# Three projection tiles taken group by group beside the first norm, squares and small loads ahead of the weights

## What is computed

```python
def rmsnorm(x, g):
    xf = x.astype(jnp.float32)
    y = xf * lax.rsqrt(jnp.mean(xf * xf, axis=-1, keepdims=True) + NORM_EPS)
    return (y * g.astype(jnp.float32)).astype(x.dtype)
...
    h = rmsnorm(x, g_pre)
    proj = h @ w_in
    u, q, k, v, o, gi, gf, ga, gb = jnp.split(proj, IN_SPLITS, axis=-1)
    y_a = jax.nn.gelu(s5_ssm(u, lam_re, lam_im, b_re, b_im, c_re, c_im, d, log_dt))
...
    dt = jnp.exp(log_dt.astype(jnp.float32))[:, None]
    mag = jnp.exp(lam_re * dt)
    ab_re = mag * jnp.cos(lam_im * dt)
    ab_im = mag * jnp.sin(lam_im * dt)
```

## Time and profile before

| | |
|---|---|
| time, median of 3 runs | 3489.06 us (3487.95 to 3490.17) |
| the profiled execution | 3492.63 us, span of its core 3490.8 us |
| PE busy | 3255.0 us, 93% of the span |
| DVE busy | 1745.0 us, 50% |
| ACT busy | 1203.0 us, 34% |
| chain that ended last | PE 80%, DVE 12%, ACT 5% |

### The profile page before, as it was taken

One profiled execution on the slowest core, in us unless ns is written; L12 is line 12 of the kernel. 1 busy time (PEld: TensorE's weight loads), 2 busy tenths in 40 slices (PEclk: granted clock), 3 DMA queues, 4 the chain that ended last, 5 costly groups with the idle time before them and its releaser, 6 DMA issues.

```text
span 3490.8 us, 55107 instructions
## 1 busy us (share of the span) xinstructions
PE 3255.0 (93%) x23686; PEld 2709.5 (78%) x23686; DVE 1745.0 (50%) x3048; ACT 1203.0 (34%) x2065; POOL 75.8 (2%) x124
## 2 busy tenths in 40 slices
PE   6899988889999999999999898978888999999998
PEld 4788877769878888888777776767677788888887
DVE  7656252345574243446765545454545653434355
ACT  4233353452543221224533222433434431212133
POOL 0000000001000000000000000000000000000000
PEclk9999999999999999999999999989899999999999
DMA  2111121224322111123443122000002221111133
GB/s 102 68 62 65 65 92 61 74 89 131 139 95 86 55 41 52 38 76 127 148 167 120 65 70 83 11 29 29 11 20 91 85 96 62 47 50 46 51 97 109
DMA packets 85234, 262.28 MB, mean 75 GB/s; under 512 B 10208, under 2 KB 10336, under 8 KB 84864
## 3 DMA queue, kind: packets, MB, share of 16 engines
q1 hardware_dynamic: 73056, 217.78, 18.8%
q0 software_dynamic: 7040, 23.16, 1.9%
q10 hardware_dynamic: 4896, 17.84, 1.3%
HBM read 216.51 MB, written 42.21 MB: 74 GB/s over the span
## 4 chain that ended last, share of the span: by engine, by line
PE 80%; DVE 12%; ACT 5%; issue 2%; DMA 1%; DVEq 0%; SPq 0%; POOL 0%; ACTq 0%; POOLq 0%
PE ps L127 77%; DVE HB L161 2%; PE ps L130 2%; PE ps L126 2%; DVE w_lo L161 1%; ACT L140 1%; ACT w_hi L158 1%; DVE HB L171 1%; ACT m_D L140 1%; DVE r_t L161 1%; DVE r_in L161 0%; DVE C L171 0%; DMA w_raw<-in_w_u 0%; DVE r_Xa L161 0%; DMA m_D<-mq 0%
## 5 line engine op out<-in xcount | busy, mean ns | idle before, releaser
L161 DVE TENSOR_TENSOR w_lo<-w_raw,w_hi 128x1024 fp32r<-128x1024 f32 (+3 forms) x353 | 393.5, 1115 | 388.3 <-ACT w_hi L158 386.1
L127 PE MATMUL ps<-XHA,w_hi 128*128 128x264 f32 (+3 forms) x1456 | 474.5, 326 | 24.6 <-ACT HB L158 9.2
L127 PE MATMUL ps<-XLA,w_hi 128*128 128x264 f32 (+3 forms) x1456 | 462.8, 318 | 0.0
L127 PE MATMUL ps<-XHA,w_lo 128*128 128x264 f32 (+3 forms) x1456 | 460.7, 316 | 0.0
L158 ACT ACTIVATE w_hi<-w_raw 128x1024 fp32r<-128x1024 f32 (+3 forms) x353 | 339.7, 963 | 320.5 <-PE ps L127 281.3
L127 PE MATMUL ps<-XHB,w_hi 128*128 128x512 f32 x920 | 381.0, 414 | 10.2 <-issue 6.0
L127 PE MATMUL ps<-XLB,w_hi 128*128 128x512 f32 x920 | 364.2, 396 | 0.0
L127 PE MATMUL ps<-XHB,w_lo 128*128 128x512 f32 x920 | 364.1, 396 | 0.0
L127 PEld LDWEIGHTS ps<-XHA,w_hi 128*128 128x128 f32 x1456 | 281.5, 193 | 55.4 <-issue 31.2
L127 PEld LDWEIGHTS ps<-XLA,w_hi 128*128 128x128 f32 x1456 | 281.6, 193 | 21.8 <-issue 4.1
L127 PEld LDWEIGHTS ps<-XHA,w_lo 128*128 128x128 f32 x1456 | 281.8, 194 | 16.5
(11 more groups left out here) (440 smaller groups left out, 6045.6 us busy)
## 6 DMA issues: line engine op xcount, KB each, us to landing
w_raw<-in_f_gate SPq DMA_DIRECT2D x66, 512.0 KB, 3.3
w_raw<-in_f_up SPq DMA_DIRECT2D x66, 512.0 KB, 3.3
w_raw<-in_w_out SPq DMA_DIRECT2D x32, 512.0 KB, 3.4
w_raw<-in_f_down SPq DMA_DIRECT2D x48, 320.0 KB, 2.9
w_raw<-in_f_down SPq DMA_DIRECT2D x32, 384.0 KB, 3.1
w_raw<-in_w_rkv SPq DMA_DIRECT2D x24, 512.0 KB, 3.3
w_raw<-in_w_attn SPq DMA_DIRECT2D x24, 512.0 KB, 4.0
w_raw<-in_w_qkvo SPq DMA_DIRECT2D x16, 512.0 KB, 3.4
```

Source lines behind the costliest of these rows:

```text
L127: return Issued(e.matmul(out, a, b, start=start, stop=stop))
L161: return Issued(self.eng and self.eng.tensor_tensor(out, a, b, op))
```

## The change

Nothing is computed otherwise; instructions are moved.

- SP: ssm_p1 and ssm_p2 are issued first. Then SP waits until x tile 3 has landed, and issues weights 0 and 1 and ssm_bc1 (on a semaphore of its own, `ssm_bl`, for which DVE waits at its use).
- ACT and DVE: splits 0, 1 and 2 leave the front. Split 0 comes behind the squares of k = 5, split 1 behind those of k = 6, split 2 behind the first group of the norm.
- ACT makes roots 0 and 1 before the norm, root 2 behind the first group. DVE waits for each root where its group begins.
- PE takes u0, u1 and u2 together: first group of tokens of all three, then the second, then the third (`FIRST`), nine groups in eight banks, as numbers 4 to 7 use the ring K.sb and the rest K.fg. u3 and all others go as before.
- ACT copies the nine groups out in this order. Both ACT and DVE advance their background work by one tick a group as before, but the splits 3, 4 and 5 now come behind the 7th, 8th and 9th group, where they came behind the 3rd, 6th and 9th. (`next_tile` is called where c is 2.)

```diff
+FIRST_W = (5, 6)
...
 def prenorm_act(A, K):
...
         A.step(K0)
+        if k in FIRST_W:
+            split_act(A, K, FIRST_W.index(k))
...
+    root(0)
+    root(1)
     for c, (c0, cn) in enumerate(CH1):
         normalise_act(A, K, S, c, c0, cn, K.tmp1)
+        if c == 0:
+            root(2)
+            split_act(A, K, 2)
...
 def prenorm_dve(V, K):
     S = K.pn
-    V.step(8 * K0)
+    for k in range(8):
+        V.step(K0)
+        if k in FIRST_W:
+            split_dve(V, K, FIRST_W.index(k))
...
     for c, (c0, cn) in enumerate(CH1):
+        V.wait_ge(S.act, ("sd", c))
         normalise_dve(V, K, S, K.HB, K.rs0, c, c0, cn, "g_mix_pre", K.tmp1)
+        if c == 0:
+            split_dve(V, K, 2)
...
 def ssm_sp(D, K):
     D.dma(K.ssm_p1[:, :, :], K.I["ssm_p1"]).then_inc(K.ssm_ld, by=16)
-    D.dma(K.ssm_bc1[:, :, :, :], K.I["ssm_bc1"]).then_inc(K.ssm_ld, by=16)
     D.dma(ssm_views(K).p2, K.I["ssm_p2"]).then_inc(K.ssm_ld, by=16)
+    D.wait_ge(K.x[3], "x")
+    load_weight(D, K, 0)
+    load_weight(D, K, 1)
+    D.dma(K.ssm_bc1[:, :, :, :], K.I["ssm_bc1"]).then_inc(K.ssm_bl, by=16)
...
+FIRST = [(c, t) for c in range(3) for t in range(3)]
+def first_ring(K, n):
+    return K.sb if 4 <= n < 8 else K.fg
+def first_pe(P, K, ready):
+    S = K.in1
+    tiles = [next_tile(P, K, None) for _ in range(3)]
+    shape = lambda t: t[:, :].rearrange("p (k n) -> p k n", k=8)
+    for n, (c, t) in enumerate(FIRST):
+        i, (c0, cn) = tiles[t], CH1[c]
+        wh, wl = shape(K.his[i]), shape(K.los[i])
+        P.wait_ge(K.w.act, ("hi", i))
+        P.wait_ge(K.w.dve, ("lo", i))
+        b = first_ring(K, n).take(P, ("u", t, c))
...
+def first_act(A, K):
+    S = K.in1
+    next_tile(A, K, split_act)
+    for n, (c, t) in enumerate(FIRST):
+        (c0, cn), ring = CH1[c], first_ring(K, n)
+        A.wait_ge(S.pe, ("u", t, c))
+        A.cp(by_phase(K.HB[:, 4 + t, 0:T1], c0, cn), blocks8(ring["u", t, c][:, 0:cn])).then_inc(S.act, ("u", t, c))
+        ring.done(("u", t, c), S.act, ("u", t, c))
+        A.tick()
+        A.u_done += c == 2
+        if c == 2 and t < 2:
+            next_tile(A, K, split_act)
+def first_dve(V, K):
+    next_tile(V, K, split_dve)
+    for c, t in FIRST:
+        V.tick()
+        V.u_done += c == 2
+        if c == 2 and t < 2:
+            next_tile(V, K, split_dve)
...
 def in1_pe(P, K):
     ready = normalised(P, K.pn)
-    for name, m in IN1:
+    first_pe(P, K, ready)
+    for name, m in IN1[3:]:
         dense(P, K, K.in1, name, m, 8, K.X, ready, CH1)
```

More of the change, by code:

```diff
@@ L463, in prenorm_act, with root @@
         A.step(K0)
+        if k in FIRST_W:
+            split_act(A, K, FIRST_W.index(k))
     A.table(LN_EXP)
-    for c, (c0, cn) in enumerate(CH1):
+    def root(c):
+        c0, cn = CH1[c]
         A.wait_ge(S.pe, ("sq", 7, c))
@@ L468, in prenorm_act @@
         K.fg.done(("pn", "sum", c), S.act, ("sd", c))
+    root(0)
+    root(1)
     for c, (c0, cn) in enumerate(CH1):
         normalise_act(A, K, S, c, c0, cn, K.tmp1)
+        if c == 0:
+            root(2)
+            split_act(A, K, 2)
 def prenorm_dve(V, K):
     S = K.pn
-    V.step(8 * K0)
+    for k in range(8):
+        V.step(K0)
+        if k in FIRST_W:
+            split_dve(V, K, FIRST_W.index(k))
     K.tmp1.n[V] = 24
-    for c, (c0, cn) in enumerate(CH1):
-        V.wait_ge(S.act, ("sd", c))
     for k in range(8):
@@ L701, in ssm_dve @@
     V.after(d)
+    V.wait_ge(K.ssm_bl, END)
     cmul(V, d, sq(K.ssm_bb1[:, 0, :]), sq(K.ssm_bb1[:, 1, :]), b16(zr1), b16(zi1), bc1[:, 0], bc1[:, 1],
@@ L869, in spill_place @@
     return K.mo[m if name == "o" else 4 + m]
+FIRST = [(c, t) for c in range(3) for t in range(3)]
[11 more added lines that the diff above has]
+        b = first_ring(K, n).take(P, ("u", t, c))
+        for k in range(8):
+            ready(k, c)
+            x, y = K.X.hi(k, c0, cn), K.X.lo(k, c0, cn)
+            P.mm(b[:, 0:cn], wh[:, k, :], x, k == 0, False)
+            P.mm(b[:, 0:cn], wh[:, k, :], y, False, False)
+            op = P.mm(b[:, 0:cn], wl[:, k, :], x, False, k == 7)
+        op.then_inc(S.pe, ("u", t, c))
+        K.used[i] = (S.pe, ("u", t, c))
+        P.tick()
+        P.u_done += c == 2
+def first_act(A, K):
[17 more added lines that the diff above has]
+            next_tile(V, K, split_dve)
 def in1_pe(P, K):
     ready = normalised(P, K.pn)
-    for name, m in IN1:
+    first_pe(P, K, ready)
+    for name, m in IN1[3:]:
         dense(P, K, K.in1, name, m, 8, K.X, ready, CH1)
@@ L894, in in1_act @@
     behind = None
-    for name, m in IN1:
+    first_act(A, K)
+    for name, m in IN1[3:]:
         next_tile(A, K, split_act)
@@ L929, in in1_dve @@
     S = K.in1
-    for name, m in IN1:
+    first_dve(V, K)
+    for name, m in IN1[3:]:
         next_tile(V, K, split_dve)
@@ L3034, in make_signals @@
     K.pst = several("p_out", 4)
-    K.gpad, K.ssm_ld, K.m_v, K.rotl = [K.named(n) for n in ("gpad", "ssm_in", "vo_in", "rot_in")]
+    K.gpad, K.ssm_ld, K.ssm_bl, K.m_v, K.rotl = [K.named(n) for n in ("gpad", "ssm_in", "ssm_bc_in", "vo_in", "rot_in")]
     K.lora, K.a_mask, K.a_ld, K.outs = [K.named(n) for n in ("lora_in", "mask_in", "a_in", "outs")]
@@ L3228, in sync_program @@
 def sync_program(D, K):
-    load_weight(D, K, 0)
-    load_weight(D, K, 1)
     ssm_sp(D, K)
@@ L3274, in act_program @@
     A.step()
-    for i in range(3):
-        split_act(A, K, i)
     A.wait_ge(K.c.pool, END)
@@ L3303, in dve_program @@
     V.step()
-    for i in range(3):
-        split_dve(V, K, i)
     V.wait_ge(K.c.cst, END)
```

## The result

The changed kernel takes 3496.19 us (median of 16 runs), the kernel before 3490.07 us (median of 16 runs beside them). The ratio is 1.0020, 95% interval 1.0013 to 1.0027: 6 us slower by the medians, 7 us by the ratio, whose interval reaches from 4.5 to 9.4 us. Forecast were 3494.7 and +5.6 us. The profiled execution of the changed kernel has a span of 3494.9 us against 3490.8. In one of the experiments (e1) PE was granted 0.674 of its clock for a whole profiled execution; its rows are taken from a second profile of the same kernel, e8.

The account below looks back on a forecast made before the run. PE's start of tile v0 was taken as bound by DVE's chain (discretisation, norm, powers). Terms -9.25 + 4.6 + 3.14 - 2.27 gave -3.8, plus 9.4 for PE's wait: +5.6, 3494.7 us; range 3490.5 to 3498.5.

Parts of the forecast that it names:

- first square: ACT's first square, after x tile 0 landing at 8.6 and the table load: at 9.95, -9.25 us.
- splits 0 and 1 in the discretisation: DVE stands for w_hi and does w_lo between the sine steps, about 2.55 and 2.0 us: together +4.6 us.
- root 2 and split 2 inside the norm: DVE waits for ACT's root 2 and w_hi 2, then does w_lo 2 before the second group: +3.14 us.
- powers without w_lo 3 and 4: Both w_lo now stand behind DVE's last ssm_W row, so the powers take 2.27 us less.
- PE's restart: PE, through at about 77, stands until w_lo 3 is done at 104.8, then does u3.
- The step that gave the forecast its sign: u3 needs w_lo 3, which DVE reaches only after the powers: 12.72 us come on, 3.34 leave, +9.4 us.
- The sign named for it: In the profile, PE idle from about 77 to 104.8, ended by DVE w_lo, 27 us long.
- Rival (c): PE held only by v0's bank, copied after ssm_Bop, not by w_lo 3: -3.8, 3485.3 us; chance 0.04.
- Rival (d): Neither w_lo 3 nor the bank holds PE; whole overlap counts, u2 ending at 77: -12.9, 3476 us; chance 0.05.
- The slow start: PE's lower clock at the restart after the gap: one such start in each kernel, priced 0.
- Rival (a): x tiles land some 2.5 us apart, ACT waits about 2.7 us for x4: +8.3, 3497.4 us; chance 0.17.
- Rival (b): Delay taken back later, where a stage behind PE has another bound: +2, 3491 us; chance 0.12.

Follow-up runs that it names:

- e1: Changed kernel with loads, weight splits 0 to 2 and roots as in the kernel before, leaving only the order by groups: 3498.85 us, ratio 1.0025.
- e8: The kernel of e1 once more, unchanged, profiled for its rows alone; no time given.
- e4: Changed kernel with splits 0 and 1 behind the squares on ACT and behind the discretisation on DVE: 3492.01 us, ratio 1.0005.
- e3: Changed kernel with w_lo 3 and 4 behind DVE's first two state-space ticks, w_hi 4 ahead of ACT's ssm_Bop copies: 3490.68 us, ratio 1.0003.
- e10: Changed kernel with ACT's copies into ssm_Bop one tick later, behind all nine banks and w_hi 4: 3497.12 us, ratio 1.0019.
- e5: Changed kernel with w_lo 3 to 7 earlier, ACT's ssm_Bop copies eight ticks later, first state-space round three ticks later: 3465.4 us, ratio 0.9926.
- e2: Changed kernel with projection tiles one after the other as in the kernel before; loads and early splits as changed: 3489.72 us, ratio 0.9995.
- e7: e2 with w_lo 3 to 7 earlier, ssm_Bop copies seven ticks later, first state-space round three ticks later: 3479.2 us, ratio 0.9967.
- e6: e5 with splits 0 and 1 behind the discretisation: 3465.7 us, ratio 0.9927.
- e9: e5 with loads, splits 0 to 2 and roots as in the kernel before: 3472.37 us, ratio 0.9948.

## Why the prediction was right

The terms, as the prediction put them and as the rows of the changed kernel have them:

| term | forecast, us | measured, us |
|---|---|---|
| first square | 9.95 | 9.56 |
| splits 0 and 1 in the discretisation | +4.6 | +4.54 |
| the rest from first square to norm | 0 | +0.43 |
| norm start | 38.35 | 38.33 |
| root 2 and split 2 inside the norm | +3.14 | +2.97 |
| powers without w_lo 3 and 4 | -2.27 | -2.04 |
| powers end | 103.5 | 103.52 |
| PE's restart | 104.8 | 104.76 |
| PE's gap | 77 to 104.8 | 77.14 to 104.76 |
| v0's third group against before | +5.6 | +5.80 |
| time | +5.6 | +6.1 by the medians, +7.0 by the ratio (4.5 to 9.4) |

**First square.** x tile 0 ended the wait at 8.2, 0.4 us before the value taken (8.6). The landing row of the eight x tiles in the changed kernel (from issue, the first issued at 1.3):

```profile
DMA to landing us min/median/max: 6.9/9.4/13.1
```

By the estimate from the Trainium skill, "DMA: Bandwidth & Descriptors", section "Anatomy of one DMA — SWDGE (gpsimd) path", it would have come at 6.9, ahead of vecs; the trace has 1.3 + 6.9 = 8.2 for it and 1.2 + 6.5 = 7.7 for vecs, so it came last. That estimate was 1.3 us early and the row of the kernel before (9.3) 1.1 us late; 8.6, taken between them, was 0.4 late.

**Splits between the sines.** From first square to norm it was 43.00 - 19.20 = 23.80 us before and is 38.33 - 9.56 = 28.77 now, 4.97 more. The splits have their two stretches: from the first sine to the second 2.56 us before and 28.61 - 23.53 = 5.08 now (+2.52, worked out 2.55), and from the second sine to DVE's row on ssm_a 35.72 - 35.20 = 0.52 before and 31.15 - 28.61 = 2.54 now (+2.02, worked out 2.0). DVE stood 1.43 us before each of the two w_lo, as worked out. The other 0.43 us isn't the splits'. Ahead of the first sine 0.53 came on: ACT waits for PE to have taken a square at 16.03 and at 17.78, where in the kernel before it did so once, and PE's first squares took that much longer. These are the first and the fourth row of them, now, and the fourth row before, whose first was at 19.75:

```profile
10.12 2.10 PE L127 MATMUL ps<-ssm_VX,cst 128*128 128x264 f32 x4 [10.12 <-ACT ssm_VX L140]
...
15.83 1.05 PE L127 MATMUL ps<-ssm_VX,cst 128*128 128x264 f32 x4
```

```profile
24.95 1.05 PE L127 MATMUL ps<-ssm_VX,cst 128*128 128x264 f32 x4
```

That is 5.71 us now and 5.20 before. The two misses ahead of the norm, -0.39 for the first square and +0.37 for the way from there, cancel: that the norm's start came out to 0.02 us is luck. e4 took the two stands away and moved the norm by 2.13 us where 2.3 were expected.

**Split 2 in the norm.** 47.71 - 38.33 = 9.38 us between the first two groups, against 6.41 before: +2.97, 0.17 less than forecast. From DVE's first row behind the norm to the end of the powers it is 103.52 - 64.54 = 38.98 us now and 41.02 before, so that leaving out the two w_lo gave 2.04 us and not 2.27; nothing shows why. These two misses cancel as well.

**What PE waits for.** The step that gave the forecast its sign was right: w_lo 3 stands behind the powers and u3 behind w_lo 3. e3 shows it by taking it away, e10 by leaving it alone. The sign named for it, a gap that the profile puts down to DVE's w_lo, did not come: the profile says "issue", and it took the experiments. Rival (c), that only the bank holds PE, is what e3 makes of the kernel and not what the change is: its v0 starts at 109.79, and the bank's wait then costs 20.50 us. The -3.8 us given to (c) was not reached there: v0 started 109.79 - 110.59 = -0.8 us from its old place, as e3 has the two w_lo back among the powers (2.3 us) and its norm started at 39.15, 0.8 us later than in the changed kernel. Rival (d), the whole overlap, needs w_lo 3 early and ssm_Bop late together, as e5 has them. Its price was too low: 12.9 us, where e5 gained 26. It counted only the earlier end of u2 and left in the 9.20 us that PE stood behind u3 and the 2.1 us of the slow start of v0.

**The slow start.** I priced it alike in both kernels. From the restart to the third group it took 7.97 us before (110.59 to 118.56) and 8.27 now (104.76 to 113.03), where 124.36 - 118.51 = 5.85 us is the settled pace, so it costs 2.1 and 2.4 us. The granted clock is 0.50 in both starts (104.7 to 109 now, 110.5 to 115 before), the lower of the two levels. The difference of 0.3 us was not in the sum. On the other side PE restarted 104.76 - 103.52 = 1.24 us behind the powers and not 1.38; together with the powers' end this makes 5.80 instead of 5.6.

**The rest.** Rival (a), slow x tiles, fell: no x tile but the first made ACT wait, and the last landed at 5.1 + 13.1 = 18.2, where it had been 23.5 before. Rival (b), a delay taken back later, has something in one profile (the spans differ by 4.1 us, not 5.8), but nothing in the ratio of 16 runs (7 us). That part is noise between executions or a small effect of either sign; it was not followed further. Nor can the runs tell +5.6 from +7.0: that the time agrees with the forecast is shown to some 2.5 us, and the finer agreement is one of rows in single profiles.

## What to carry to other kernels

An engine that runs its program in order passes every wait on to what is written behind it. So a change that lets PE run ahead must also be followed into the other engines' programs: which instruction of theirs does PE need next, and what long chain is now written ahead of it? Here PE stood for 27 us behind one 1.2 us instruction, and a second wait of 20 us stood hidden behind the first; moving both, with the state-space round behind them (e5), turned a loss of 7 us into a gain of 26. A cover that costs nothing under a slow load (the first weight splits) becomes a term of the sum as soon as the load is early.

## What was not expected of the hardware

The same instruction order started its norm at times 1.6 us apart in six profiles. The loads are not the reason: the first squares on ACT stood between 9.41 and 9.68 in all six. What differs is the time that PE took for its first squares, for which ACT waits (in e3, 0.40, 0.70 and 0.43 us before three of its squares). All in us; the fourth row is the one shown above at 15.83:

| profile | PE's first square | its fourth row | between them | norm start | norm behind the fourth row |
|---|---|---|---|---|---|
| changed kernel | 10.12 | 15.83 | 5.71 | 38.33 | 22.50 |
| e2 | 10.13 | 16.14 | 6.01 | 38.64 | 22.50 |
| e3 | 10.13 | 16.65 | 6.52 | 39.15 | 22.50 |
| e5 | 10.06 | 15.08 | 5.02 | 37.59 | 22.51 |
| e7 | 10.25 | 16.64 | 6.39 | 39.15 | 22.51 |
| e10 | 9.97 | 15.09 | 5.12 | 37.60 | 22.51 |

So the spread arises entirely ahead of PE's fourth row, and what follows repeats to 0.01 us. The first four matmuls take 2.10 us, the four of the same shape at 15.83 take 1.05; the profile's clock column reads 1.00 over both, so it doesn't show what slowed them. Counted from the fourth row, e4 and e6 both start the norm at 20.09, so that taking the splits out from between the sines gains 2.41 us, where the starts themselves gave 2.13 and 1.18; and the norm of e9 (18.06) stands just where the kernel before has it (18.05). A sum that counts from the first load can't be better than about a microsecond, and a single profile can't tell an edit of 1 us at the norm unless it is counted from such a row.

PE's slow start after a gap hardly grew with the gap: 2.1 us lost behind 9.20 us idle, 2.4 us behind 27.62. The Trainium skill, "TensorE: Matmul & The Clock Gate", section "What's actually happening", gives two clocks, 1.2 and 2.4 GHz. The rows have a slow and a fast pace, too. PE of the changed kernel, two matmuls in a row after the restart and two in the settled stretch:

```profile
105.56 0.42 PE L127 MATMUL ps<-XHA,w_hi 128*128 128x264 f32 x1
105.78 0.42 PE L127 MATMUL ps<-XLA,w_hi 128*128 128x264 f32 x1
...
118.63 0.28 PE L127 MATMUL ps<-XLA,w_hi 128*128 128x264 f32 x1
118.75 0.28 PE L127 MATMUL ps<-XHA,w_lo 128*128 128x264 f32 x1
```

Their starts are 0.22 us apart at first, where the granted clock is 0.50, and 0.12 us later, where it is 1.00, for the same 264 columns: 1.2 and 2.2 columns in a nanosecond. The slow pace agrees with 1.2 GHz; the fast one comes out some 8% under 2.4, and no row here says why.
